# Two moves in the HGRN2 head steps of a two-layer block kernel: a vector readout ahead of the first level, and weight-piece loads paired in the DMA queue

## The chip, the cores and the metric

One NeuronCore of a Trainium2 chip runs the whole program, in one launch. The metric is device microseconds of one execution. Shorter is better. Engines are named as in the profile: PE (TensorE), DVE (VectorE), ACT (ScalarE), POOL (GpSimd), SP (SyncE, which here only issues DMAs).

## The reference

The reference is two layers of a transformer-like trunk on 256 context tokens and 512 latent tokens of width 1024, in float32. Layer 0 mixes tokens with a bidirectional gated linear recurrence (HGRN2, 8 heads of 128), layer 1 with windowed attention; each is followed by a gated feed-forward with a 3x3 convolution. What the change touches is inside layer 0's mixer and the modulation vector that both layers use:

```
q, i_in, gate, zf = split(x @ w_in)            # 5 x 128 columns for one head, two decay directions in zf
log_f = log(lb + (1 - lb) * sigmoid(zf));  k = (1 - lb) * sigmoid(-zf)
o     = chunked scan over tokens, forward and backward, of  S = diag(exp g) S + k v^T,  o = S^T q
out   = (rms_norm(o per head, norm_g) * silu(gate)) @ w_out
mod   = silu(c) @ ada_w + ada_b                # 6 x 1024 values for a layer: shift, scale and gate of its parts
```

## The kernel before

**Products.** Activations lie transposed, channels on partitions and 768 tokens along the row. Every product with a weight is done in three passes: activation and weight are each split into a rounded part and a rest (HH and HL, WH and WL), and `products` (lines 399 to 401) adds high by high, low by high and high by low. A weight tile is 1024 x 128. SP loads it (`WR<-in_w`, line 330), ACT makes WH (line 786, in `split_high`), DVE makes WL (line 1085, in `split_low`), PE uses it. There are three buffers of each, and tile t is loaded when tile t-3 has been used.

**Head steps.** The mixer goes through eight head steps, numbered 0 to 7 here, of about 71 us each. In step h, PE works on the recurrence of head h, on the tail of head h-1 (its states, its output, its normalization) and on the projection of head h+1. That projection is five weight tiles, tiles 5h+5 to 5h+9, cut into ten half tiles, n = 0 to 9; between two half tiles PE does one piece of the recurrence (`between(n)`). Step 0 has no tail, step 7 has no projection; in step 7 PE does products of the output matrix in its place. The recurrence of a head is a tree of seven levels. For each level PE multiplies queries with keys (`level_scores`, line 526; a first one without level, line 524) into one PSUM tensor, MA, and DVE merges the masked result into PS (`take`, line 1293). The next scores are written over MA only when `take` is done (semaphore `scores_read`). Around this, DVE rescales keys (`merge_keys`, lines 1254 and 1255), queries (`merge_queries`, 1265 and 1266) and totals (1281), and ACT copies the mixed keys (`mix_keys`, 872).

**The tail's readout.** PE sums the squares of head h-1 in `between(2)` (line 491), ACT takes the root, DVE the reciprocal (1158), PE spreads it over the partitions in `between(3)` (line 497, semaphore `rstd_spread`), and DVE multiplies twice in `head_out` (1316 and 1318, semaphore `y_ready`). PE waits for `y_ready` in `between(4)`.

**Pieces of ada_w.** The modulation vector is computed in small portions that are strewn over PE's work. In every head step PE uses four pieces of ada_w, numbered 0 to 3 here, in `between(5)` to `between(8)` (`ada_piece`, lines 452 and 453). A piece is two halves of 128 x 512, so a step has halves 0 to 7. SP loads a half into one of two buffers `ada_raw` (line 325) and, before it issues that load, waits until the half before the last has been split. POOL splits a half (lines 356 and 358) into one of two pairs of buffers, and waits until PE has used the half before the last. SP issues everything in one order, and a table, `pieces_after`, says after which weight tile's load how many pieces stand. A wait of SP therefore holds up all loads that stand behind it.

**In-order engines.** ACT's order in a step puts `split_high` of tile 5h+10, the first of the next step, before it empties the projection of tile 5h+8, that is after `mix_keys` of level 4. DVE's order has `split_low` of that tile between `take` of level 3 and `merge_keys` of level 4.

Of the kernel before, what the change touches and what calls it, by code (L numbers as in the profile page):

```python
# [60 lines left out]
ADA_FIRST = 4  # L61
# [37 lines left out]
def trunk(nc, small_in, x_in, ada_in, w_in, ident_in, masks_in, rope_in, rot_in, tri_in, out):  # L99
    ctx = ExitStack()  # L100
    with ctx:
# [178 lines left out]

        def pieces_after():

            after, n, t = {}, 4 * ADA_FIRST, 5
            for h in range(HEADS - 1):
                after[t + 2], after[t + 5], after[t + 6] = 2, 1, 1
                t += 5
            after[t + 2] = 4
            t = T_FF0 + 4
            for g, chunks in enumerate(GROUPS):
                for j in range(2 * chunks - 4 * (g == 0)):  # L290
                    after[t + j] = 1
                t += 2 * chunks - 4 * (g == 0)
                if g < 2:
                    for j in range(2, 6):
                        after[t + j] = 1
                t += KC
            assert n + sum(after.values()) == 4 * ADA_GROUPS
            return after

        PIECES = pieces_after()  # L300

        block = ctx.enter_context(nc.Block())
# [770 lines left out]
        def _(dve):  # L1073
# [7 lines left out]
            def split_low(last):  # L1081
                while low.now() <= min(last, TILES - 1):
                    t = low.now()
                    dve.wait_ge(w_hi_done, t + 1)
                    tt(WL[t % NB][:, :, :], WR[t % NB][:, :, :], WH[t % NB][:, :, :].bitcast(F32), ALU.subtract).then_inc(w_split, 1)  # L1085
                    low.add()
# [9 lines left out]
            def link(ins):  # L1096
                mark(ins)
                settle()
# [23 lines left out]
            def ada_add(j):  # L1122

                dve.wait_ge(ada_turned, rows.now())
                tt(ada[:, j:j + 4, :], MB[:, 512:520].rearrange("p (m v) -> p m v", v=2),
                   ada_b[:, j:j + 4].unsqueeze(2).to_broadcast([P, 4, 2]), ALU.add).then_inc(ada_ready, 1)
# [28 lines left out]
            def token_rstd(first):  # L1155
                stats.add()
                dve.wait_ge(std_ready, stats.now())
                nc.vector.reciprocal(rstd6[:, first:NCH], std6[:, first:NCH]).then_inc(rstd_ready, 1)
# [69 lines left out]
            def forget(b, parity, h):  # L1228

                tile.add(2)  # L1230
                dve.wait_ge(evacuated[parity], tile.half())
                tile.add()
                dve.wait_ge(evacuated[1 - parity], tile.half())
                tile.add(2)
                f = FD[b][:, :, :].rearrange("p d t -> p (d t)")
                link(ts(f, f, oml[:, h:h + 1], lbv[:, h:h + 1], ALU.mult, ALU.add))

            def decayed_queries(b):

                mark(tt(QQ[b][:, :, :], Q[:, :].unsqueeze(1).to_broadcast([P, 2, TOK]), FD[b][:, :, :], ALU.mult))  # L1240

            def diagonal(b):

                level.add()
                tt(KL[1][:, :], KK[b][:, 0, :], KK[b][:, 1, :], ALU.add).then_inc(level_ready, 1)

            def merge_keys(b, n):

                s = 2 ** n
                settle()  # L1250
                mixed.add()
                dve.wait_ge(keys_mixed, mixed.now())
                k, f = KK[b], FD[b]
                tt(half(k, 0, s, 0), half(k, 0, s, 0), spread_totals(f, FORE, s, 1), ALU.mult)
                last = tt(half(k, 1, s, 1), half(k, 1, s, 1), spread_totals(f, BACK, s, 0), ALU.mult)  # L1255
                last.then_inc(keys_ready, 1)
# [3 lines left out]
            def merge_queries(b, n, done):  # L1260

                s = 2 ** n
                dve.wait_ge(scores_done, done)
                q, f = QQ[b], FD[b]
                tt(half(q, FORE, s, 1), half(q, FORE, s, 1), spread_totals(f, FORE, s, 0), ALU.mult)
                last = tt(half(q, BACK, s, 0), half(q, BACK, s, 0), spread_totals(f, BACK, s, 1), ALU.mult)
                if n < LEVELS - 1:
                    level.add()
                    last.then_inc(level_ready, 1)
                else:  # L1270
                    last.then_inc(kq_final, 1)

            def merge_totals(b, n):

                if n < LEVELS - 1:
                    dve.wait_ge(level_ready, level.now())
                else:
                    dve.wait_ge(kq_final, head.now())
                s = 2 ** n
                for plane in (FORE, BACK):  # L1280
                    mark(tt(total(FD[b], plane, s, 0), total(FD[b], plane, s, 0), total(FD[b], plane, s, 1), ALU.mult))
# [3 lines left out]
            def take(n):  # L1285

                taken.add()
                dve.wait_ge(scores_done, taken.now())
                if taken.some(1):
                    dve.wait_ge(scores_read, taken.now(1))  # L1290
                for c in range(2):
                    t = slice(c * TOK // 2, (c + 1) * TOK // 2)
                    last = nc.vector.copy_predicated(  # L1293
                        PS[:, t].rearrange("p (c t) -> p c t", t=P), masks[:, n:n + 1, :].to_broadcast([P, NCH // 2, P]),
                        MA[:, PC0 + t.start:PC0 + t.stop].rearrange("p (c t) -> p c t", t=P))
                last.then_inc(scores_read, 1)

            def states(b):

                settle()  # L1300
                for n, (st, plane, src, order) in enumerate(((SF, FORE, MB, FWD), (SB, BACK, MA, BWD))):
                    dve.wait_ge(kv_done, head.times(2, n - 1))
                    for j, c in enumerate(order[:-1]):
                        kv = src[:, PC0 + c * P:PC0 + (c + 1) * P]
                        if j == 0:
                            ins = cp(st[:, 0, :], kv)
                        else:
                            ins = stt(st[:, j, :], st[:, j - 1, :], FD[b][:, plane, c * P:c * P + 1], kv, ALU.mult, ALU.add)
                        if j < NCH - 2:
                            link(ins)  # L1310
                    ins.then_inc(states_ready, 1)

            def head_out(h):

                dve.wait_ge(rstd_spread, stats.now())
                link(tt(O1[:, :], O1[:, :], MB[:, PC0:PE0], ALU.mult))
                y = Y[:, h:h + 1, :].rearrange("p o t -> p (o t)")
                tt(y, y, O1[:, :], ALU.mult).then_inc(y_ready, 1)

            def gate(s, h):  # L1320
                dve.wait_ge(gate_sig, gates.add().now())
                y = Y[:, h:h + 1, :].rearrange("p o t -> p (o t)")
                tt(y, y, SLOT[s][:, HG0:HG1], ALU.mult).then_inc(evacuated[s], 1)
# [3 lines left out]
            def head_step(b, parity, h, j0, tail=True, project=True):  # L1327
                forget(b, parity, h)
                first = tile.now()
                decayed_queries(b)  # L1330
                if project:
                    split_low(first + 2)
                if tail:
                    states(1 - b)
                diagonal(b)
                if tail:
                    token_rstd(0)
                head.add()
                take(LEVELS)
                for n in range(LEVELS):  # L1340
                    merge_keys(b, n)
                    if tail and n == 0:
                        head_out(h - 1)
                    merge_queries(b, n, taken.now() + 1)
                    take(n)
                    merge_totals(b, n)
                    if project and n in (0, 2, 3, 4):
                        split_low(first + (3 if n == 0 else n + 2))
                rows.add()
                ada_add(j0)  # L1350
                if project:
                    gate(parity, h + 1)
# [6 lines left out]
            gate(0, 0)  # L1359
            j0 = 4 * ADA_FIRST  # L1360
            head_step(0, 1, 0, j0, tail=False)

            for i in range(3):
                head_step(1, 0, i * 2 + 1, i * 8 + (j0 + 4))
                head_step(0, 1, i * 2 + 2, i * 8 + (j0 + 8))
# [247 lines left out]
```

## Time and profile before

| what | value |
|---|---|
| median of 3 runs | 2151.58 us (2151.53 to 2157.55) |
| the profiled execution | 2151.58 us, of which 2149.8 us from the first to the last instruction |
| PE busy | 2009.3 us, 93% of the span |
| DVE busy | 1337.0 us, 62% |
| ACT busy | 704.1 us, 33% |
| POOL busy | 430.8 us, 20% |
| chain that ended last | PE 76%, DVE 14%, ACT 4%, DMA 3% |
| mean granted TensorE clock | 0.958 of full speed |
| head steps 0 to 7 | from about 105 us to 660 us of the span |

The share of busy time of PE is an upper bound, since the ends of matmuls are modelled and matmuls overlap. A row of the timeline gives the start in us from the span's start, the duration in us of a merged run of like instructions, the engine, the line of the code, the operation, what is written and read, and, in brackets, how long the engine was idle before and who ended that. Float32 matmuls show twice in a count (x12 for six).

### The profile page before, as it was taken

How to read it: one execution, taken by the hardware profiler on the slowest of the kernel's cores; microseconds unless marked ns; L12 is line 12 of the kernel's file. 1: busy time of each engine (PE TensorE's matmuls, PEld its weight loads, DVE VectorE, ACT ScalarE, POOL GpSimd, SP SyncE). 2: the span in 40 equal slices, each digit the busy share in tenths (PEclk: the TensorE clock that was granted, in tenths of full speed). 3: DMA queues.
4: the chain of work that ended last, by engine and by line, in shares of the span. 5: the costliest groups of instructions: out<-in, count | busy, mean ns of one | idle time of the engine just before them, and what ended most of it. 6: DMA issues, size and time to landing. Idle time of an engine off the chain costs nothing.

```text
span 2149.8 us, 26437 instructions
## 1 busy us (share of the span) xinstructions
PE 2009.3 (93%) x10776; PEld 1678.4 (78%) x10776; DVE 1337.0 (62%) x2043; ACT 704.1 (33%) x1065; POOL 430.8 (20%) x342
## 2 busy tenths in 40 slices
PE   5999999999988899999999999799899879999997
PEld 2999999999877778888888888675565667777875
DVE  5476676667773677626772575665356378478485
ACT  5333323333322332212221223345245333233242
POOL 2032332223270034335443450000000000000000
PEclk8999999999998899999999999889989989999998
DMA  6122221222211133323323332110000113232333
GB/s 262 53 75 69 69 79 52 67 69 79 68 31 40 40 102 115 91 96 108 116 91 98 108 110 77 62 40 1 30 30 1 59 59 89 88 98 80 98 88 98
DMA packets 56856, 165.85 MB, mean 77 GB/s; under 512 B 6176, under 2 KB 6560, under 8 KB 56608
## 3 DMA queue, kind: packets, MB, share of 16 engines
q1 hardware_dynamic: 56736, 164.17, 24.0%
q8 instruction: 85, 1.39, 0.3%
q14 instruction: 35, 0.29, 0.0%
HBM read 162.05 MB, written 2.10 MB: 76 GB/s over the span
## 4 chain that ended last, share of the span: by engine, by line
PE 76%; DVE 14%; ACT 4%; DMA 3%; issue 2%; POOL 1%; SPq 0%; DVEq 0%; POOLq 0%
PE slot L399 19%; PE slot L401 19%; PE slot L400 18%; DVE ACC L1403 6%; PE slot L721 3%; PE MA L526 3%; DVE WL L1085 2%; PE MB L452 2%; PE slot L712 1%; PE MB L453 1%; ACT WH L786 1%; PE MB L497 1%; PE MB L445 1%; DMA AD<-in_ada 1%; DMA WR<-in_w 1%
## 5 line engine op out<-in xcount | busy, mean ns | idle before, releaser
L399 PE MATMUL slot<-HH,WH 128*128 128x256 f32 (+2 forms) x2016 | 722.4, 358 | 42.4 <-DVE ACC L1411 14.3
L400 PE MATMUL slot<-HL,WH 128*128 128x256 f32 (+2 forms) x2016 | 710.2, 352 | 0.0
L401 PE MATMUL slot<-HH,WL 128*128 128x256 f32 (+2 forms) x2016 | 709.8, 352 | 0.0
L399 PEld LDWEIGHTS slot<-HH,WH 128*128 128x128 f32 x2016 | 386.3, 192 | 103.9 <-issue 46.5
L1085 DVE TENSOR_TENSOR WL<-WR,WH 128x1024 fp32r<-128x1024 f32 x204 | 298.8, 1466 | 237.2 <-ACT WH L786 235.6
L400 PEld LDWEIGHTS slot<-HL,WH 128*128 128x128 f32 x2016 | 386.4, 192 | 41.2 <-issue 2.2
L401 PEld LDWEIGHTS slot<-HH,WL 128*128 128x128 f32 x2016 | 385.6, 191 | 38.6
L786 ACT ACTIVATE WH<-WR 128x1024 fp32r<-128x1024 f32 x204 | 215.2, 1056 | 368.3 <-DMA WR<-in_w 368.2
L356 POOL TENSOR_SCALAR ada_high<-ada_raw 128x512 fp32r<-128x512 f32 x160 | 140.5, 878 | 820.7 <-PE MB L453 479.3
L1403 DVE SCALAR_TENSOR_TENSOR ACC<-UP,cw,ACC 128x512 f32<-128x512 f32 x352 | 292.9, 832 | 8.6
L358 POOL TENSOR_TENSOR ada_low<-ada_raw,ada_high 128x512 fp32r<-128x512 f32 x160 | 261.5, 1635 | 13.4
L399 PE MATMUL slot<-GH,WH 128*128 128x512 f32 (+1 forms) x528 | 191.3, 362 | 8.4 <-DVE GL L1416 8.4
L401 PE MATMUL slot<-GH,WL 128*128 128x512 f32 (+1 forms) x528 | 191.2, 362 | 0.0
L400 PE MATMUL slot<-GL,WH 128*128 128x512 f32 (+1 forms) x528 | 190.6, 361 | 0.0
L990 ACT ACTIVATE ACC<-ACC 128x768 f32<-128x768 f32 (+1 forms) x44 | 32.5, 739 | 272.1 <-DVE ACC L1403 272.1
L399 PEld LDWEIGHTS slot<-GH,WH 128*128 128x128 f32 x528 | 100.5, 190 | 27.0 <-DVE GL L1416 9.7
L400 PEld LDWEIGHTS slot<-GL,WH 128*128 128x128 f32 x528 | 100.6, 190 | 17.1
L401 PEld LDWEIGHTS slot<-GH,WL 128*128 128x128 f32 x528 | 100.7, 191 | 16.1
L526 PE MATMUL MA<-QQ,KL 128*128 128x128 f32 x672 | 90.9, 286 | 4.4 <-DVE PS L1293 4.4
L526 PEld LDWEIGHTS MA<-QQ,KL 128*128 128x128 f32 x672 | 87.1, 192 | 6.3 <-issue 6.2
L872 ACT ACTIVATE KL<-KK 128x384 f32<-128x384 f32 x112 | 53.4, 526 | 106.8 <-DVE KK L1255 103.1
L452 PE MATMUL MB<-ada_high,silu_p 128*4 128x512 f32 x160 | 65.7, 410 | 11.6 <-POOL ada_low L358 11.5
(182 smaller groups left out, 2178.1 us busy)
## 6 DMA issues: line engine op xcount, KB each, us to landing
WR<-in_w SPq DMA_DIRECT2D x204, 512.0 KB, 3.6
ada_raw<-in_ada SPq DMA_DIRECT2D x160, 256.0 KB, 2.7
AD<-in_ada SPq DMA_DIRECT2D x3, 2048.0 KB, 22.8
X<-in_x SPq DMA_DIRECT2D x1, 3072.0 KB, 18.8
AD<-in_ada SPq DMA_DIRECT2D x4, 512.0 KB, 6.2
out<-Y SPq DMA_DIRECT2D x8, 256.0 KB, 2.2
Y<-in_masks SPq DMA_DIRECT2D x1, 512.0 KB, 26.0
rope<-in_rope SPq DMA_DIRECT2D x1, 512.0 KB, 3.4
```

Source lines behind the costliest of these rows:

```text
L356: pool.tensor_scalar(AH[f][:, :], AR[f][:, :], 1.0, 0.0, ALU.mult, ALU.add).then_inc(piece_hi, 1)
L358: pool.tensor_tensor(AL[f][:, :], AR[f][:, :], AH[f][:, :].bitcast(F32), ALU.subtract).then_inc(piece_split, 1)
L399: mm(SLOT[s][:, po], WH[w % NB][:, k, :], hi[:, k, to], start=(k == 0), stop=False)
L400: mm(SLOT[s][:, po], WH[w % NB][:, k, :], lo[:, k, to], start=False, stop=False)
L401: last = mm(SLOT[s][:, po], WL[w % NB][:, k, :], hi[:, k, to], start=False, stop=(k == kn - 1))
L452: mm(MB[0:4, 0:512], silu_p[:, 2 * k + f, :], AH[f][:, :], start=(k == 0 and f == 0), stop=False)
L526: last = mm(MA[:, chunk(c)], KL[n % 2][:, t], of_level(QQ[b], c * P, P, 2 ** n), start=True, stop=True)
L721: last = mm(SLOT[1][64 * half:64 * half + 64, 0:512], AV[:, c, 64 * half:64 * half + 64], PT[v % 2][:, j, :, :].rearrange("p r q -> p (r q ...
L786: go(WH[t % NB][:, :, :], WR[t % NB][:, :, :], ACT.Copy).then_inc(w_hi_done, 1)
L872: last = go(k, half(KK[b], plane, s, plane), ACT.Copy)
L1085: tt(WL[t % NB][:, :, :], WR[t % NB][:, :, :], WH[t % NB][:, :, :].bitcast(F32), ALU.subtract).then_inc(w_split, 1)
L1403: ins = stt(acc, lat[:, dy:dy + GRID_H, dx:dx + GRID_W], cw[b][:, k:k + 1], acc, ALU.mult, ALU.add)
```

## The change

Two things are done, both in the head steps.

First, the table of ada_w loads is rewritten. Before, in step h, two pieces stood behind the load of tile 5h+7, one behind tile 5h+10 and one behind tile 5h+11. Now two pieces stand behind tile 5h+8 and two behind tile 5h+9. For step 7 the four pieces stand behind tile 41 instead of tile 42. The number of pieces is the same.

Second, DVE's `head_out(h - 1)` stands right behind the reciprocal, ahead of `take(LEVELS)` and `merge_keys(b, 0)`; before, it stood behind them. PE's, ACT's and POOL's programs are unchanged.

```diff
         def pieces_after():
 
-            after, n, t = {}, 4 * ADA_FIRST, 5
+            after, n, t = {}, 4 * ADA_FIRST, 7
             for h in range(HEADS - 1):
-                after[t + 2], after[t + 5], after[t + 6] = 2, 1, 1
+                for j in range(5):
+                    after[t + j - 1] = 2 * (j in (2, 3))
                 t += 5
-            after[t + 2] = 4
+            after[t - 1] = 4
             t = T_FF0 + 4
...
                 diagonal(b)
                 if tail:
                     token_rstd(0)
+                    head_out(h - 1)
                 head.add()
                 take(LEVELS)
                 for n in range(LEVELS):
                     merge_keys(b, n)
-                    if tail and n == 0:
-                        head_out(h - 1)
                     merge_queries(b, n, taken.now() + 1)
```

On SP, in the middle head steps, where `WR<-in_w` is the load of a weight tile and each `ada_raw<-in_ada` is a half of a piece, the rows of one period before are these (the first row holds tiles 5h+8, 5h+9 and 5h+10, the next ones tiles 5h+11 and 5h+12):

```order
L330 DMA WR<-in_w 128x1024 x3
L325 DMA ada_raw<-in_ada 128x512 x2
L330 DMA WR<-in_w 128x1024
L325 DMA ada_raw<-in_ada 128x512 x2
L330 DMA WR<-in_w 128x1024
L325 DMA ada_raw<-in_ada 128x512 x4
```

The same period now (the first row is tile 5h+9, the last tiles 5h+10 to 5h+13):

```order
L326 DMA ada_raw<-in_ada 128x512 x4
L331 DMA WR<-in_w 128x1024
L326 DMA ada_raw<-in_ada 128x512 x4
L331 DMA WR<-in_w 128x1024 x4
```

In the second piece the lone tile load is tile 5h+9, and tile 5h+10 now stands behind all eight halves of the step; before, it stood behind the first four only.

On DVE, at the start of the levels in a step with a tail, the rows before are these (KL is the sum of keys that the first scores read, PS what `take` writes, O and Y the readout of the head before):

```order
L1245 TENSOR_TENSOR KL<-KK 128x768
L1158 RECIPROCAL rstd<-std 128x6
L1293 COPY_PREDICATED PS<-masks,MA 128x384 x2
L1254 TENSOR_TENSOR KK<-KK,FD 128x384
L1255 TENSOR_TENSOR KK<-KK,FD 128x384
L1316 TENSOR_TENSOR O<-O,MB 128x768
L1318 TENSOR_TENSOR Y<-Y,O 128x768
L1265 TENSOR_TENSOR QQ<-QQ,FD 128x384
```

And now:

```order
L1246 TENSOR_TENSOR KL<-KK 128x768
L1159 RECIPROCAL rstd<-std 128x6
L1317 TENSOR_TENSOR O<-O,MB 128x768
L1319 TENSOR_TENSOR Y<-Y,O 128x768
L1294 COPY_PREDICATED PS<-masks,MA 128x384 x2
L1255 TENSOR_TENSOR KK<-KK,FD 128x384
L1256 TENSOR_TENSOR KK<-KK,FD 128x384
L1266 TENSOR_TENSOR QQ<-QQ,FD 128x384
```

The two readout multiplications moved up over four instructions, of which the two COPY_PREDICATED are those that free MA for PE.

## Rows read from the trace of the kernel before

**Rows 1.** Windows, steps 1 to 6 and step 7: length, then busy time by engine

```profile
core 0: us, PE busy (x) PEld busy (x) DVE busy (x) ACT busy (x) POOL busy (x), PEclk, DMA share, GB/s
166.00:592.00 426.00, 412.87 (x2721) 396.54 (x2720) 293.72 (x488) 144.62 (x210) 128.26 (x97) 1.00 0.21 68
592.00:660.00 68.00, 56.66 (x361) 49.66 (x358) 46.21 (x85) 13.99 (x23) 38.14 (x30) 0.90 0.08 24
```

**Rows 2.** Waits of PE in steps 0 to 6: us in total, times, longest

```profile
PE MB L452 <- POOL ada_low L358: 10.9, 7, 1.8
```

**Rows 3.** Timeline of PE around n = 3 of step 3

```profile
333.06 1.50 PE L497 MATMUL MB<-ident,rstd 128*128 128x128 f32 x12
334.40 2.15 PE L526 MATMUL MA<-QQ,KL 128*128 128x128 f32 x12
```

**Rows 4.** Timeline of DVE in the same stretch

```profile
329.07 1.07 DVE L1293 COPY_PREDICATED PS<-masks,MA 128x384 f32<-128x384 uint8 x2 [0.95 <-PE MA L524]
334.60 0.95 DVE L1316 TENSOR_TENSOR O<-O,MB 128x768 f32<-128x768 f32 x1 [3.55 <-PE MB L497]
335.59 0.96 DVE L1318 TENSOR_TENSOR Y<-Y,O 128x768 f32<-128x768 f32 x1
```

**Rows 5.** Timeline of SP's queue in the second half of step 3

```profile
347.06 0.33 SPq L330 DMA_DIRECT2D WR<-in_w  x1
351.32 2.38 SPq L325 DMA_DIRECT2D ada_raw<-in_ada  x2
359.92 0.33 SPq L330 DMA_DIRECT2D WR<-in_w  x1
360.29 0.91 SPq L325 DMA_DIRECT2D ada_raw<-in_ada  x2
```

**Rows 6.** Timeline of POOL, halves 4 to 7 of step 3

```profile
356.41 1.48 POOL L358 TENSOR_TENSOR ada_low<-ada_raw,ada_high 128x512 fp32r<-128x512 f32 x1
357.87 0.62 POOL L356 TENSOR_SCALAR ada_high<-ada_raw 128x512 fp32r<-128x512 f32 x1
358.57 2.27 POOL L358 TENSOR_TENSOR ada_low<-ada_raw,ada_high 128x512 fp32r<-128x512 f32 x1
...
364.38 0.63 POOL L356 TENSOR_SCALAR ada_high<-ada_raw 128x512 fp32r<-128x512 f32 x1 [3.54 <-DMA ada_raw<-in_ada]
...
368.18 1.45 POOL L358 TENSOR_TENSOR ada_low<-ada_raw,ada_high 128x512 fp32r<-128x512 f32 x1
```

**Rows 7.** Timeline of ACT: WH of tile 5h+10 in step 3

```profile
356.25 1.05 ACT L786 ACTIVATE WH<-WR 128x1024 fp32r<-128x1024 f32 x1
```

**Rows 8.** Timeline of DVE: WL of tile 5h+10 in step 3, and what follows

```profile
358.49 1.21 DVE L1085 TENSOR_TENSOR WL<-WR,WH 128x1024 fp32r<-128x1024 f32 x1
359.63 1.63 DVE L1254 TENSOR_TENSOR KK<-KK,FD 128x384 f32<-128x384 f32 x1
```

**Rows 9.** Timeline of DVE, one level in step 7: first key merge, and `take`

```profile
619.69 0.56 DVE L1254 TENSOR_TENSOR KK<-KK,FD 128x384 f32<-128x384 f32 x1
...
621.57 1.04 DVE L1293 COPY_PREDICATED PS<-masks,MA 128x384 f32<-128x384 uint8 x2
```

**Rows 10.** Timeline of PE at n = 8 of step 3: scores of level 5, piece 3

```profile
366.15 1.50 PE L526 MATMUL MA<-QQ,KL 128*128 128x128 f32 x12
...
369.68 0.40 PE L452 MATMUL MB<-ada_high,silu_p 128*4 128x512 f32 x1 [1.57 <-POOL ada_low L358]
```

**Rows 11.** The page's DMA issues: KB each, median us to landing

```profile
WR<-in_w SPq DMA_DIRECT2D x204, 512.0 KB, 3.6
ada_raw<-in_ada SPq DMA_DIRECT2D x160, 256.0 KB, 2.7
```

**Rows 12.** Windows: two gaps of PE, and the 3.4 us after each

```profile
589.02:591.60 2.58, 0.00 (x0) 0.03 (x1) 2.58 (x8) 0.05 (x1) 0.06 (x1) 1.00 0.78 289
592.90:596.30 3.40, 3.27 (x16) 2.96 (x15) 1.62 (x3) 1.16 (x2) 3.32 (x3) 0.51 0.02 5
652.90:655.50 2.60, 0.01 (x1) 0.01 (x1) 2.32 (x8) 0.00 (x0) 0.00 (x0) 1.00 0.00 0
655.50:658.90 3.40, 3.40 (x30) 3.40 (x31) 0.00 (x0) 0.00 (x0) 0.00 (x0) 1.00 0.00 0
```

## The prediction, made before the changed kernel ran

> **What bounds the kernel now.** I read first the windows of the head steps, because the change is only there. In steps 1 to 6 PE is busy 412.87 of 426.00 us, 97%, at a granted clock of 1.00; DVE is busy 293.72, 69% [rows 1]. So PE sets the pace, every gap that the change puts into PE's row lengthens the kernel by that gap, and DVE time matters only where PE waits for it. Step 7 is different: PE is busy 56.66 of 68 us there [rows 1]. Next I read PE's waits. In steps 0 to 6 the largest is for POOL's split of the last piece: 10.9 us over seven times, one in each step, 1.56 us on average [rows 2]. That is all that a better order of the piece loads can give. Last I read the timelines of one step, number 3, engine by engine, and laid the new orders over them; the steps repeat, and I multiply.
>
> **Part 1, the readout ahead of the first take.** The readout needs the spread of the reciprocal, which PE does only in `between(3)`, from 333.06 [rows 3]. Before, DVE used the time up to then: its first take ran at 329.07 for 1.07 us, and afterwards it was idle for 3.55 us until the spread ended that wait, at 334.60 [rows 4]. PE began the scores of level 0 at 334.40, straight behind the spread [rows 3], since MA had been freed long ago. Now the take stands behind the readout, and PE may not write MA before it. The chain is: readout starts 334.60, its second multiplication starts 335.59 and takes 0.96, so 336.55 [rows 4]; then the take, 1.07, so 337.62; then some 0.1 for PE to start. PE starts level 0 at about 337.7 instead of 334.40: 3.3 us later. Nothing hides it: behind the scores on PE stand the half tile n = 4 and all the rest, and PE has no work that it could put first. What gets late next? The query merge waited for nobody before and now waits for the later scores, so DVE keeps its old distance to PE, and no second wait follows at level 1. The early y_ready buys nothing, as no row of PE shows a wait on it in steps 1 to 6. There are seven steps with a tail: 7 x 3.3 = 23 us. In step 7, where DVE is closer to the bound, I count the same. Bounds: 3.0 us (no start-up, the shortest handing over) to 4 us (a take or multiplication slowed by POOL) for each, 21 to 28 us.
>
> **Part 2, the pieces paired.** The queue of SP is the thing to follow. The load of a half waits until the half before the last is split, and POOL's split waits for PE's use of the half before the last. Halves 4 and 5 can't be issued before PE's n = 5, and the last half, 7, is issued only when half 5 is split, which needs PE's use of half 3 at n = 6. Before, this did no harm: the load of tile 5h+10 was already out at 347.06, at the end of n = 5 [rows 5]. Now it stands behind half 7. POOL: half 4 was split by 357.89, half 5 started at 357.87, its second instruction at 358.57 [rows 6]. That one took 2.27 us beside DVE's work on the tile and the keys [rows 8]; now DVE will be waiting, so I take 1.3 as the short end, between the 1.45 and 1.48 of the other rows [rows 6] and what a free POOL may do: 359.9. Half 7 is issued, and 0.37 later (the distance of 359.92 and 360.29 in [rows 5]) the tile: 360.3, which is 13 us later than before. It takes 3.6 [rows 11], and about 0.5 more since a 256 KB half went just ahead of it (estimate: the two sizes differ by 0.9 us in landing, less the 0.37 of head start) [rows 11]: 364.4. ACT converts for 1.05 [rows 7], 365.5, where it started at 356.25 before. DVE's split of the tile takes 1.21 [rows 8]: 366.7, where it ended at 359.7. Behind it in DVE's order stand the merges and the take of level 4, together 621.57 + 1.04 - 619.69 = 2.9 us when POOL is quiet [rows 9]: 369.6. PE wants to write MA with the scores of level 5 at 366.15 [rows 10] and starts at 369.7: a new gap of 3.5 us. Against it, piece 3 is now split in good time (half 7 is issued near 359.9 instead of 361, and half 6 before it does not wait behind a tile load; before, its split began only at 364.38 and the last ended at 369.63 [rows 6]), so the old wait of 1.57 at 369.68 [rows 10], 1.56 on average, goes. Net 3.5 - 1.56 = 1.9 us a step. ACT's late emptying of tile 5h+8 is covered, PE needs that PSUM only in the next step. Steps 0 to 6 have it: 7 x 1.9 = 13.6 us. In step 7 the four pieces only hold up tile 42, which is needed after the step. Bounds: the gap is 2.4 us if the tile lands like an undisturbed one and DVE is quicker than in the rows, and 5.6 if POOL's 2.27 stays and the merges run as slowly as the 1.63 of [rows 8]; net 0.8 to 4 us, 6 to 28 us in all.
>
> The same rows bear on a rule. POOL's instruction takes 2.27 us instead of 1.48 and DVE's key merge 1.63 instead of 0.56 where they overlap [rows 6, 8, 9]. The Trainium skill, page "SBUF — State Buffer", section "Who interferes with whom", says that a vector instruction with two SBUF inputs and a GpSimd instruction that reads SBUF hold each other up. The trace agrees in kind. By this rule the new order should help DVE, since halves 0 and 1 are split while DVE is idle, around n = 2, and no longer at a step's start; what that would be worth is a rival below.
>
> **Part 3, the clock.** Two new gaps of over 3 us come into every step. In step 7 a gap of 2.58 us was followed by 3.4 us at a granted clock of 0.51, that is 1.2 instead of 2.4 GHz; a gap of 2.60 us was followed by 1.00 [rows 12]. Steps 1 to 6 have no such gap and stay at 1.00 [rows 1]. Of six gaps of 2.3 to 3.9 us in the span that stand apart from other idle time (these rows show one of either kind), five were followed by such a stretch, so I take it that 8 of 10 new gaps bring one, and that it costs nearly half of its length, 1.6 us, as PE is the bound there: 14 gaps x 0.8 x 1.6 = 18 us. Bounds: 0 (no gap brings it) and 14 x 1.6 = 23, or twice that if stretches last twice as long.
>
> **Sum.** 23 + 13.6 + 18 = 55 us on the profiled execution's 2151.58 us, which is the median too: 2206 us, 2.5% slower.
>
> **The rivals.** *Gaps without the clock.* The two waits come as said but the clock stays: 2151.6 + 37 = 2188 us. For it: the gap of 2.60 us in [rows 12]. Against it: the other gap there, which is shorter than the new ones.
>
> *Only the readout costs.* The tile's late load is swallowed, because its landing or DVE's slack is better than in my chain, and the piece wait is gone: 23 - 10.9 + 7 x 0.8 x 1.6 = 21 us, 2173 us. For it: a chain of seven links, each of which can be half a microsecond shorter. Against it: it must be 3.5 us shorter in all.
>
> *Worse than forecast.* The merges behind the late tile fall on POOL's splits of halves 6 and 7, and the slow clock lasts two stretches: 28 + 28 + 30 = 86 us, 2237 us at the far end, 2225 as a typical value. For it: POOL and DVE do slow each other in [rows 6, 8]. Against it: POOL should be through with half 7 near 366.
>
> *Faster: POOL's relief.* The pieces come in time, the 10.9 us are won, and POOL's splits fall into DVE's idle time, so that DVE is ahead of PE everywhere: 2151.6 - 10.9 = 2141 us. This decides itself at one point: the first take must be done before PE wants to start level 0, at 334.40, though the readout ahead of it waits for the spread that PE issues only then. The spread can't be earlier, as PE does it behind the half tile n = 3. By the skill's rule on the shared port DVE gains time here; but DVE's gain lies where PE doesn't wait. I see hardly a way for it. A piece wait that stays, so that the change doesn't do what its table suggests, would add the 11 us again to the forecast and lies in the range.
>
> **How the numbers follow.** Forecast, both waits and the clock: 0.48, with its own range 2193 to 2218. Without the clock 0.20, only the readout 0.15, worse 0.12, faster or no change 0.05. The time is the likeliest case's, 2206. The range reaches down to 2173, which takes in the case of the readout alone at its centre, and up to 2226: about 0.15 is left outside. A difference of 0.3%, 6.5 us, is what this kernel's measurement can tell from none. Below 2145 lies most of the rival that is faster, 0.03; within 0.3%, 0.02, if three terms happen to cancel; slower 0.95.
>
> **What would show it.** Step 1 of the argument: PE waits at line 526 for DVE's take (line 1294 now) seven times at level 0, for 3 us or so, and DVE's readout starts right behind the spread. If those waits aren't there, part 1 is wrong. Step 2: SP issues the load of tile 5h+10 some 13 us later in the step, DVE sits idle for about 6 us before line 1086 with ACT's WH as the releaser, ACT before line 787 with the DMA, and PE waits again at line 526 at n = 8; the wait of line 452 on POOL is gone or under 1 us in total. Step 3: the granted clock in steps 1 to 6 falls from 1.00 to about 0.9 or a little above. The head steps 1 to 6 should take about 47 us more than 426. If the kernel is not slower, the reading that PE can't go past a late take is wrong, and with it most of this text.

## The result, and the profile after

The changed kernel took 2215.8 us (median of 4 runs, 2215.4 to 2218.75), the kernel before 2154.41 us in the same session. The ratio is 1.0288, 95% interval 1.0266 to 1.0309: 61 us slower. The forecast was 2206 us, in a range of 2173 to 2226.

Windows of both kernels first: steps 0 to 6, of before and then of after (the columns are those of [rows 1]).

```profile
105.00:590.00 485.00, 471.61 (x3083) 452.65 (x3082) 335.31 (x552) 163.50 (x240) 147.68 (x112) 1.00 0.22 70
```

```profile
105.00:645.00 540.00, 493.87 (x3089) 469.83 (x3087) 303.10 (x548) 164.21 (x241) 118.89 (x118) 0.95 0.20 64
```

Nearly the same instructions take 55 us more. PE is busy 97% of the first and 91% of the second window, and its granted clock fell from 1.00 to 0.95. DVE's busy time shrank by 32 us and POOL's by 29 for nearly the same instructions. It comes with the table (`e2_table_only` has DVE busy for 303.16 us in steps 0 to 6 too), and the long rows of DVE beside POOL in [rows 6, 8] suggest that the two get in each other's way less than before; it bought nothing. The feed-forward and attention stages did the same work in 1481 and 1484 us, so nothing of note happened there.

The waits of PE in steps 0 to 6 of the changed kernel (us in total, times, longest), which answer to [rows 2]:

```profile
PE MA L527 <- DVE PS L1294: 44.6, 13, 4.3
PE MB L550 <- ACT RF L891: 1.5, 6, 0.2
```

The wait for POOL, 10.9 us before, is gone. In its place PE waits 13 times for DVE's `take`, once at level 0 in steps 1 to 6 and once at level 5 in steps 0 to 6. Step 3 shows both. First PE and DVE at level 0, to be held against [rows 3, 4]:

```profile
357.23 1.50 PE L498 MATMUL MB<-ident,rstd 128*128 128x128 f32 x12
361.82 2.90 PE L527 MATMUL MA<-QQ,KL 128*128 128x128 f32 x12 [3.09 <-DVE PS L1294]
```

```profile
358.77 0.95 DVE L1317 TENSOR_TENSOR O<-O,MB 128x768 f32<-128x768 f32 x1 [6.48 <-PE MB L498]
359.76 0.96 DVE L1319 TENSOR_TENSOR Y<-Y,O 128x768 f32<-128x768 f32 x1
360.63 1.04 DVE L1294 COPY_PREDICATED PS<-masks,MA 128x384 f32<-128x384 uint8 x2
```

DVE is idle for 6.48 us and does the take only when PE already wants MA. PE starts 4.59 us after the spread's first matmul; before it was 334.40 - 333.06 = 1.34: 3.25 us later. Second, the chain to level 5: SP, ACT, DVE and PE, which answer to [rows 5], [rows 7], [rows 8] and [rows 10].

```profile
379.75 8.88 SPq L326 DMA_DIRECT2D ada_raw<-in_ada  x4
388.68 0.91 SPq L331 DMA_DIRECT2D WR<-in_w  x2
```

```profile
393.11 1.06 ACT L787 ACTIVATE WH<-WR 128x1024 fp32r<-128x1024 f32 x1 [8.33 <-DMA WR<-in_w]
```

```profile
386.05 0.95 DVE L1282 TENSOR_TENSOR FD<-FD 128x48 f32<-128x48 f32 x2
394.20 1.23 DVE L1086 TENSOR_TENSOR WL<-WR,WH 128x1024 fp32r<-128x1024 f32 x1 [7.20 <-ACT WH L787]
...
397.22 1.04 DVE L1294 COPY_PREDICATED PS<-masks,MA 128x384 f32<-128x384 uint8 x2
```

```profile
398.41 2.11 PE L527 MATMUL MA<-QQ,KL 128*128 128x128 f32 x12 [3.66 <-DVE PS L1294]
```

Tile 5h+10 is issued at 388.68, behind the last half. ACT waits 8.33 us for it, DVE 7.20 us for ACT, and PE 3.66 us for DVE. The half ahead of the tile could be issued only when POOL had split half 5, whose second instruction is this one:

```profile
387.00 1.29 POOL L359 TENSOR_TENSOR ada_low<-ada_raw,ada_high 128x512 fp32r<-128x512 f32 x1
```

Two windows of 3.4 us, from where PE starts again, show the granted clock, in the last column but two (0.55 and 0.63; parts of them are at full speed again):

```profile
361.40:364.80 3.40, 2.98 (x13) 3.01 (x14) 1.23 (x4) 1.00 (x2) 0.00 (x0) 0.55 0.02 5
398.40:401.80 3.40, 3.39 (x16) 2.41 (x17) 3.37 (x7) 0.94 (x2) 0.00 (x0) 0.63 0.00 0
```

In step 7 there is one more thing that the prediction had no term for, PE's wait for DVE's gate product at its start:

```profile
PE MB L544 <- DVE Y L1324: 5.2, 1, 5.2
```

Before, that wait was 2.6 us. The waits for `take` in step 7 are these, before and after:

```profile
PE MA L526 <- DVE PS L1293: 4.4, 4, 1.8
PE MA L527 <- DVE PS L1294: 6.5, 3, 3.1
```

The new one at level 0 is 3.1 us, and two small ones of before are gone: 2.1 us net.

The granted clock was also read over all head steps in windows of half a microsecond each. In steps 0 to 6 of the changed kernel every one of the 13 gaps has a stretch at half speed that begins within it or behind it, ten of 3.4 us and three of 6.8 us, 54.6 us together. In some 5 us of these PE was still idle (by windows of a quarter of a microsecond). Step 7 has 20.5 us of slow clock, before 13.7.

### The profile page after: what moved, and what is told of

Read it like the earlier page. It is cut to its first block, busy times and chain, and to the rows that moved or that the text cites. A ratio compares the mean times of both kernels' runs of the same rounds, so it can differ in the third digit from the quotient of the medians.

```text
span 2215.5 us, 26437 instructions
## 1 busy us (share of the span) xinstructions
PE 2034.7 (92%) x10776; PEld 1695.0 (77%) x10776; DVE 1305.8 (59%) x2043; ACT 704.2 (32%) x1065; POOL 395.8 (18%) x342
## 4 chain that ended last, share of the span: by engine, by line
PE 73%; DVE 16%; ACT 4%; DMA 3%; issue 2%; POOL 1%; SPq 0%; DVEq 0%; POOLq 0%
PE slot L400 18%; PE slot L402 17%; PE slot L401 17%; DVE ACC L1403 6%; PE MA L527 4%; PE slot L722 3%; DVE WL L1086 3%; DMA WR<-in_w 2%; PE MB L453 2%; PE MB L454 1%; ACT WH L787 1%; PE slot L713 1%; PE MB L498 1%; PE MB L446 1%; DMA AD<-in_ada 1%
## 5 line engine op out<-in xcount | busy, mean ns | idle before, releaser
L1086 DVE TENSOR_TENSOR WL<-WR,WH 128x1024 fp32r<-128x1024 f32 x204 | 292.1, 1433 | 278.4 <-ACT WH L787 276.8
L357 POOL TENSOR_SCALAR ada_high<-ada_raw 128x512 fp32r<-128x512 f32 x160 | 129.1, 807 | 904.1 <-DMA ada_raw<-in_ada 454.5
L359 POOL TENSOR_TENSOR ada_low<-ada_raw,ada_high 128x512 fp32r<-128x512 f32 x160 | 236.7, 1479 | 13.3
L527 PE MATMUL MA<-QQ,KL 128*128 128x128 f32 x672 | 102.8, 310 | 51.2 <-DVE PS L1294 51.1
L527 PEld LDWEIGHTS MA<-QQ,KL 128*128 128x128 f32 x672 | 96.9, 219 | 56.1 <-issue 56.0
L722 PE MATMUL slot<-PT,AV 128*64 128x512 f32 x144 | 74.8, 670 | 1.4 <-ACT PT L1033 1.4
```

The costliest lines, as they stand in the source:

```text
L357: pool.tensor_scalar(AH[f][:, :], AR[f][:, :], 1.0, 0.0, ALU.mult, ALU.add).then_inc(piece_hi, 1)
L359: pool.tensor_tensor(AL[f][:, :], AR[f][:, :], AH[f][:, :].bitcast(F32), ALU.subtract).then_inc(piece_split, 1)
L527: last = mm(MA[:, chunk(c)], KL[n % 2][:, t], of_level(QQ[b], c * P, P, 2 ** n), start=True, stop=True)
L722: last = mm(SLOT[1][64 * half:64 * half + 64, 0:512], AV[:, c, 64 * half:64 * half + 64], PT[v % 2][:, j, :, :].rearrange("p r q -> p (r q ...
```

## The experiments

All ratios are to the kernel before, timed in the same session; its medians there were 2154.93 us (first four) and 2155.28 us (last four). In the diffs, the lines left out are as in the kernel before, unless the text says so.

**One edit at a time.** The theory was that the two edits make two separate waits. The rival for the first kernel was that they lose time only together, for the second that the pairing of pieces is good in itself.

`e1_readout_only`:

```diff
                 if tail:
                     token_rstd(0)
+                    head_out(h - 1)
                 head.add()
                 take(LEVELS)
...
-                    if tail and n == 0:
-                        head_out(h - 1)
```

> Only the readout stands early, the table of pieces is that of before. My theory: seven waits of PE at the level scores for the take, 3.1 us each, 21.6 us, and a slow-clock stretch after each, 3.4 to 6.8 us long at half speed (11 to 20 us), so 33 to 42 us over the kernel before, about 2188 us; the wait for POOL at piece 3 stays at some 10 us. Rival: the two edits lose time only together (the readout makes a gap only because POOL and the late tile push DVE back); then this one is within 10 us of the kernel before.

Measured: 2181.81 us, ratio 1.0129 (1.0110 to 1.0149), 27 us slower. PE's waits in steps 0 to 6:

```profile
PE MA L526 <- DVE PS L1293: 18.5, 6, 3.1
PE MB L452 <- POOL ada_low L358: 10.3, 7, 1.6
```

The wait at level 0 is there alone, 3.1 us, and POOL's wait stays. The time is under the band of 33 to 42 us expected. The windows of half a microsecond show one slow stretch of 3.4 us behind each of the six gaps, 20.5 us in all (mean clock 0.98, window below). That is the short end of what I had put in, and each us of it costs less than half a us (see `e6_both_filled`). The rival of a joint loss is out.

`e2_table_only`:

```diff
-            after, n, t = {}, 4 * ADA_FIRST, 5
+            after, n, t = {}, 4 * ADA_FIRST, 7
             for h in range(HEADS - 1):
-                after[t + 2], after[t + 5], after[t + 6] = 2, 1, 1
+                for j in range(5):
+                    after[t + j - 1] = 2 * (j in (2, 3))
                 t += 5
-            after[t + 2] = 4
+            after[t - 1] = 4
```

> Only the table of pieces is new, the readout stands where it was. My theory: seven waits of PE before the scores of level 5, 3.5 us each, 24 us, less the 10.9 us of POOL's wait, and 11 to 20 us of slow clock, so 24 to 33 us over the kernel before, about 2181 us. Rival: the pairing is good by itself (POOL's wait gone, POOL out of DVE's way) and only the readout costs; then this one is about 11 us faster than before.

Measured: 2184.24 us, ratio 1.0138 (1.0122 to 1.0154), 29 us slower. PE's waits in steps 0 to 6:

```profile
PE MA L527 <- DVE PS L1294: 26.2, 7, 4.5
```

Seven waits of 3.7 us on average, and none for POOL; the time is as expected. Here one of the seven gaps brought no slow stretch, the one in step 4. The windows are the gap and the 3.4 us behind it:

```profile
455.50:459.00 3.50, 0.00 (x0) 0.02 (x1) 3.50 (x10) 1.88 (x3) 0.00 (x0) 1.00 0.00 0
459.00:462.40 3.40, 3.38 (x22) 2.90 (x23) 3.40 (x7) 1.24 (x3) 0.00 (x0) 1.00 0.02 5
```

The two edits alone cost 1.29% and 1.38%, together 2.67%; the changed kernel costs 2.88%. They add up within the intervals.

**Which place in the queue does the harm.** The next kernel moves the second pair of pieces one tile later; the readout is where it was.

`e3_pair_later`:

```diff
-                after[t + 2], after[t + 5], after[t + 6] = 2, 1, 1
+                after[t + 3], after[t + 5] = 2, 2
```

> The readout where it was; two pieces behind tile 5h+8 and two behind tile 5h+10 in place of 5h+9. If the harm of the new table is only that the load of tile 5h+10 stands behind halves that wait for PE, it goes completely here and the gain stays: no gap before level 5, POOL's wait under 2 us, clock at 1.00 in steps 1 to 6, 9 to 11 us faster than before, about 2142 us. Now tile 5h+11 stands behind half 7 and lands some 1.5 us later, which DVE's distance of about 3 us at level 6 should hide. Rival: it is the crowding of POOL's splits after n = 5 that delays DVE, whatever the tile does; then the gap before level 5 stays at 3 us and the kernel is slower by 20 us or more.

Measured: 2142.0 us, ratio 0.9941 (0.9923 to 0.9959): 13 us faster than before, somewhat more than the 9 to 11 expected, by less than the interval. SP in step 3 has tile 5h+10 ahead of halves 4 to 7 now:

```profile
342.00 0.33 SPq L330 DMA_DIRECT2D WR<-in_w  x1
346.26 9.87 SPq L325 DMA_DIRECT2D ada_raw<-in_ada  x4
```

In steps 0 to 6 only these waits of PE are left:

```profile
PE MB L543 <- DVE Y L1323: 2.6, 1, 2.6
PE MB L549 <- ACT RF L890: 1.5, 6, 0.2
```

The first lies at the border to step 7. The gap at level 5 is gone and POOL's wait too, so the rival (POOL's crowded splits hold DVE up) is out: the splits lie where they did (in step 3 the halves 2, 4 and 6 begin at 343.94, 350.37 and 356.80, in the changed kernel at 377.42, 383.86 and 390.28), and what moved is the tile, to ahead of the halves.

`e7_half_late` puts tile 5h+10 behind two halves instead of none or four:

```diff
-                after[t + 2], after[t + 5], after[t + 6] = 2, 1, 1
+                after[t + 3], after[t + 4], after[t + 5] = 2, 1, 1
```

> The readout where it was; two pieces behind tile 5h+8, one behind 5h+9 and one behind 5h+10. Tile 5h+10 now stands behind halves 4 and 5 alone, which can be issued when PE is at n = 5: it goes out near 353.8 of step 3 instead of 347.1 and lands near 357.5, ACT has it near 358.6, where DVE asks for it at 358.5. If only being later than DVE's need costs, then 6 to 7 us of delay cost nothing: no gap at level 5, the time of the version with the second pair two tiles later, about 2142 us. Rival: every delay of that load costs in proportion (half of the 3.5 us gap): then 10 to 15 us more than 2142.

Measured: 2140.03 us, ratio 0.9942 (0.9928 to 0.9957), the same as the one before. SP and DVE in step 3:

```profile
349.96 0.43 SPq L330 DMA_DIRECT2D WR<-in_w  x1
```

```profile
356.75 1.23 DVE L1085 TENSOR_TENSOR WL<-WR,WH 128x1024 fp32r<-128x1024 f32 x1 [1.98 <-ACT WH L786]
...
361.71 1.05 DVE L1293 COPY_PREDICATED PS<-masks,MA 128x384 f32<-128x384 uint8 x2
```

Here DVE does wait for the tile, 1.98 us, and PE doesn't: its waits for `take` in steps 0 to 6 sum to 0.4 us. So the loss is not in proportion to the delay: 1.98 us of waiting on DVE cost PE nothing, the 7.20 us of the changed kernel cost it 3.66 us. That fits a distance of some 3.5 us between DVE and PE here, an estimate from the difference of these two waits; nothing between the two points was run.

**Which neighbour of the readout.** `e4_after_take` keeps the table of before and puts the readout between the take and the key merge:

```diff
                 take(LEVELS)
+                if tail:
+                    head_out(h - 1)
                 for n in range(LEVELS):
                     merge_keys(b, n)
-                    if tail and n == 0:
-                        head_out(h - 1)
```

> The table of before; the readout stands behind the first take and ahead of the key merge, that is two instructions later than in the changed kernel. If only the take behind the readout stops PE, PE starts level 0 straight behind the spread as before, no gap, clock at 1.00; the key merge comes about 4.5 us later than before, and ACT's mixed keys for level 1 are still there in time: within 3 us of the kernel before. Rival: anything that waits for the spread ahead of the merges costs; then PE waits 1 us or more at level 1 seven times, and the kernel is 7 to 15 us slower.

Measured: 2155.64 us, ratio 1.0002 (0.9988 to 1.0016), no change, as expected. PE starts level 0 straight behind the spread:

```profile
333.34 1.50 PE L497 MATMUL MB<-ident,rstd 128*128 128x128 f32 x12
334.67 2.15 PE L526 MATMUL MA<-QQ,KL 128*128 128x128 f32 x12
```

The key merge came 6.4 us later, counted from the take (at 336.74 against 329.35 in this trace, at 330.03 against 329.07 before), more than the 4.5 expected, and cost nothing. Of the four instructions that the readout overtook, only the two of the take matter.

**The clock by itself.** If the slow stretches come from the gaps, then filling the gaps should remove them without touching the waits. PE gets matmuls that nobody uses (the wait ahead of the first ones is there so that the PSUM columns that they write have been emptied):

```diff
+            def filler(s, m):
+                for _ in range(m):
+                    mm(SLOT[s][:, 0:P], ident[:, :], ident[:, :], start=True, stop=True)
...
                         if tail:
                             head_spread()
+                            if project:
+                                pe.wait_ge(evacuated[parity], tile.half(1))
+                                filler(parity, 12)
                         level_scores(b, 0)
...
+                    if n == 8 and project:
+                        filler(parity, 13)
                     if n >= 4:
                         level_scores(b, n - 3)
```

`e5_readout_filled` is the kernel with the early readout alone and the first filler:

> The kernel with the early readout alone, and on PE, in steps 1 to 6, twelve more 128 x 128 matmuls of the identity behind the spread (12 x 0.22 = 2.7 us), written to columns of PSUM that nobody reads. They lie in the 3.1 us in which PE would wait for the take, so they delay nothing; what they change is that PE isn't idle. If the clock falls because of the gap, it stays at 1.00 in steps 1 to 6 and the six stretches of 3.4 us at half speed go: 9 to 10 us faster than the same kernel without them (2181.8), about 2172 us. Rival: the slow clock comes from something else, or the matmuls of a slow stretch cost nothing since PE waits anyway: the same time as without them, or some us more.

Measured: 2174.45 us, ratio 1.0103 (1.0087 to 1.0118), against 1.0129 without the filler. The windows of steps 1 to 6, without and with it:

```profile
166.00:615.00 449.00, 420.24 (x2706) 403.09 (x2705) 289.44 (x484) 143.43 (x207) 126.28 (x96) 0.98 0.20 63
```

```profile
166.00:610.00 444.00, 431.00 (x2865) 413.70 (x2864) 290.13 (x486) 144.63 (x210) 125.95 (x96) 1.00 0.21 65
```

The clock is back at 1.00. PE still waits for `take` behind the fillers, so they delayed nothing there:

```profile
PE MA L526 <- DVE PS L1300: 2.5, 6, 0.4
```

By the medians, 7 us are won, where 9 to 10 were expected; the difference of the ratios, 0.26%, is not much above what the intervals allow, so this one alone would not decide it.

`e6_both_filled` is the changed kernel with both:

> The changed kernel, with the same twelve matmuls at level 0 in steps 1 to 6 and thirteen (2.9 us) ahead of the scores of level 5 in steps 0 to 6, where PE waits 3.5 us. Theory: the 13 gaps no longer bring slow stretches, which were 54.6 us long together and cost nearly half of that: 24 to 27 us faster than the changed kernel (2215.8), about 2190 us; what is left over the kernel before are the waits themselves, some 35 us. Rival as for the other filled one: no gain.

Measured: 2193.29 us, ratio 1.0186 (1.0167 to 1.0205), against 1.0288 without the fillers: 22 us less, a little under the 24 to 27 expected. The two intervals together allow some 6 us either way. Its window of steps 0 to 6, beside the one of the changed kernel above:

```profile
105.00:625.00 520.00, 511.14 (x3417) 491.93 (x3415) 303.89 (x549) 163.69 (x241) 119.44 (x118) 1.00 0.21 67
```

```profile
PE MA L527 <- DVE PS L1303: 7.2, 13, 0.7
```

With PE at work in the gaps the clock stays at 1.00, and the kernel with 328 matmul records more is the faster one. All 13 waits for `take` are still there, shorter by the fillers, so PE comes to the next scores no sooner than DVE lets it. The 22 us are the price of the slow clock; what is left over the kernel before, 38 us (35 expected), fits the two kinds of wait and the start of step 7.

**The last line of the table.** `e8_last_early` is `e3_pair_later` with the four pieces of step 7 behind tile 41, as in the changed kernel:

```diff
-            after[t + 2] = 4
+            after[t + 1] = 4
```

> The table with two pieces behind 5h+8 and two behind 5h+10, and the four pieces of step 7 behind tile 41 as in the changed kernel, not 42. POOL should split the first of them in step 6 and start on the heads' outputs sooner, in DVE's way at the start of step 7: PE's wait for DVE's gate product there 5.2 us instead of 2.6, so 2 to 4 us more than 2142. Rival: no difference.

Measured: 2147.49 us, ratio 0.9963 (0.9949 to 0.9976), some 5 us over `e3_pair_later`, where 2 to 4 were expected; the intervals of the two ratios overlap a little, so the times alone would not decide it, but the wait itself grew by as much, from 2.6 to 8.0 us. The wait at the start of step 7, and why, from DVE and POOL at the end of step 6:

```profile
PE MB L543 <- DVE Y L1323: 8.0, 1, 8.0
```

```profile
576.67 2.17 DVE L1255 TENSOR_TENSOR KK<-KK,FD 128x384 f32<-128x384 f32 x1
578.76 1.17 DVE L1265 TENSOR_TENSOR QQ<-QQ,FD 128x384 f32<-128x384 f32 x1
579.85 2.15 DVE L1266 TENSOR_TENSOR QQ<-QQ,FD 128x384 f32<-128x384 f32 x1
```

```profile
576.42 2.00 POOL L367 TENSOR_TENSOR HL<-Y,HH 128x768 fp32r<-128x768 f32 x1
578.39 1.13 POOL L365 TENSOR_SCALAR HH<-Y 128x768 fp32r<-128x768 f32 x1
579.61 1.98 POOL L367 TENSOR_TENSOR HL<-Y,HH 128x768 fp32r<-128x768 f32 x1
```

In `e3_pair_later`, POOL began the heads' outputs only after the pieces, and DVE's last key merge stood alone:

```profile
585.42 0.83 POOL L365 TENSOR_SCALAR HH<-Y 128x768 fp32r<-128x768 f32 x1
```

```profile
573.49 0.55 DVE L1255 TENSOR_TENSOR KK<-KK,FD 128x384 f32<-128x384 f32 x1
```

In `e8_last_early` POOL got its piece early, went on to the heads' outputs at once, and did so while DVE was in its last levels; merges that take 0.55 us alone took 2.17 and 2.15. The Trainium skill, page "SBUF — State Buffer", section "Who interferes with whom", names this pair of engines and two-input operations of this kind as the ones that contend; the trace agrees. It also shows the limit of the rule for a forecast: what POOL leaves alone in one place it hits in another.

## Why the prediction was right

**The bound.** PE sets the pace of steps 0 to 6; this held. The 32 us of DVE time that the new table saved bought no time that the runs could show.

**Part 1, the take behind the readout: right.** Forecast seven waits of 3.3 us, 23 us; measured 3.1 us each, 18.5 in steps 1 to 6 and 3.1 in step 7, 21.6 us. In step 7 two smaller waits for `take` went in return, so 20.6 us are net; the prediction counted step 7 like the others. `e4_after_take` shows that it is the take and nothing else, and `e1_readout_only` that it needs no second edit.

**Part 2, the tile behind the halves: right, link by link.** Forecast a gap of 3.5 us; measured 44.6 - 18.5 = 26.1 us in seven, 3.7 each. In step 3 the tile was issued some 14 us later than before, with the shift of the step (357.23 - 333.06) and the 3.25 us at level 0 taken off, of which the slow clock behind that gap may be one or two; forecast 13. The second instruction of half 5's split took 1.29 us (forecast 1.3), ACT began on the tile 4.4 us after its issue (4.1), and from DVE's start on it to PE's start were 4.2 us (4.2). The old wait for POOL went as said. Net 15.2 us, forecast 13.6. `e3_pair_later` removes exactly that order and keeps the gain.

**Part 3, the clock: right in kind, somewhat small.** Forecast 18 us for 14 gaps, with 8 of 10 followed by a slow stretch of 3.4 us. Measured by the fillers, 22 us for the 13 gaps of steps 0 to 6 alone, with some 6 us of uncertainty; the windows give the same, 55 us more less 18.5 and 15.2 of waits is 21 us. What was mis-sized is the slow time for each gap: none of the 13 was spared and three brought 6.8 us, 54.6 us together, 4.2 for each gap against 0.8 x 3.4 = 2.7. The mean clock agrees (540 x 0.05 x 2 = 54). The price per us of slow stretch was lower than forecast, 22 / 54 = 0.41 against nearly one half. Part of the reason is that PE was idle in 5 us of these stretches anyway; the rest lies within the uncertainty. One sign in the prediction did not follow from its own sum: 12 gaps x 0.8 x 3.4 us at half speed in 473 us is a mean clock of 0.97, not "about 0.9". Measured were 0.95, and 52 us more for steps 1 to 6 where 47 were forecast:

```profile
171.00:649.00 478.00, 431.44 (x2718) 410.47 (x2717) 267.70 (x487) 144.53 (x210) 106.26 (x105) 0.95 0.19 61
```

**What was missing.** The prediction said that in step 7 the four pieces only hold up tile 42. They also send POOL to the heads' outputs earlier. PE's wait there doubled from 2.6 to 5.2 us in the changed kernel and in `e2_table_only`, and stayed at 2.6 in `e1_readout_only`; `e8_last_early` shows the same edit to cost some 5 us with the wait at 8.0.

**The sum.** 21.6 + 15.2 + 22 + 2.6 = 61 us, which is what the medians differ by. That it fits to the us is luck: the clock term alone is known to 6 us, and in step 7 the sum counts 1.0 us of waits too many and leaves out 6.8 us of slow clock, some 3 us at the price above. The two traces differ by 66 us. The forecast of 55 us was short by the clock and by step 7, and some 1.5 us too high in part 1 and too low in part 2, which cancels.

**The rivals.** The measured 2216 us lie near the upper end of the likeliest case's own range, 2193 to 2218. Gaps without the clock is out by the 0.95 and by `e6_both_filled`. Only the readout costs is out by `e2_table_only`. Worse than forecast came true in one part, since three slow stretches lasted twice as long; its other part did not, since the merges behind the late tile took 0.55 us each and POOL had split half 7 by 394.24, before they began. The faster one is out for this kernel, but half of it was true: the 10.9 us were to be had, with the tile ahead of the second pair. `e3_pair_later` and `e7_half_late` beat both kernels, by 13 and 15 us in the medians, 0.6% each in the ratio. That is 2 to 4 us more than the wait they remove, which is inside the intervals.

## What to carry to other kernels

Before an instruction is moved up on an in-order engine, look at what it overtakes and who waits for that: an early readout with a late input is harmless behind the take and costs 27 us ahead of it. In a queue with waits, ask of every load what stands ahead of it and when that can be issued at the earliest; a load may be late up to the distance that its user has to the bounding engine (2.0 us of waiting on DVE were free here, 7.2 us were not). Count a gap of some 3 us on TensorE as more than its length, here by 1.7 us on average.

## What the runs showed of the hardware

All 13 gaps of 3.1 to 4.3 us in the changed kernel's steps 0 to 6 brought a slow stretch of 3.4 or 6.8 us, and so did the six of 3.1 us in `e1_readout_only`. In `e2_table_only` six of seven did; the seventh, of 3.6 us, was followed by a clock of 1.00. In the kernel before, one of the two gaps of about 2.6 us in [rows 12] was not followed by one. So a gap of this length makes the slow clock likely here, not certain. Adding about 25 idle matmuls to each step made the changed kernel 22 us faster.
